# Experts ranked by token count: 20 with 64 places, 44 with 32 in four column tiles, and a row-wise first projection

## The reference

```python
s = sigmoid(t @ router_w); choice = s + router_bias
# groups of 8 experts: the 4 best of 8 groups, in them the TOP_K = 6 best experts of a token
w = take(s, eidx); w = w / sum(w) * 2.5
gates = sum(one_hot(eidx, 64) * w)
def expert_step(acc, p):
    wg, wu, wd, g = p
    hid = silu(t @ wg) * (t @ wu)              # 1024 -> 256
    return acc + (hid @ wd) * g[:, None], None # 256 -> 1024
shared = (silu(t @ sh_w_gate) * (t @ sh_w_up)) @ sh_w_down
return routed + shared
```

## Time and profile before

| | |
|---|---|
| Median of 3 runs | 1358.21 us (1357.56 to 1358.25) |
| Profiled execution | 1358.36 us, span 1356.6 us |
| TensorE busy | 1299.2 us, 96% |
| VectorE, ScalarE, GpSimd busy | 481.6, 324.2, 78.0 us |
| HBM read | 445.61 MB, 329 GB/s over the span |
| Gate and up matmuls, L925 | 446.5 us |
| Down matmuls, L947 | 233.8 us |
| Gather, L899 | 136.3 + 126.4 us |
| Scatter, L993 | 104.0 + 100.5 us |
| Mean granted TensorE clock | 0.989 |

### The profile page before, as it was taken

One profiled execution on the slowest core, in us unless ns is written; L12 is line 12 of the kernel. 1 busy time (PEld: TensorE's weight loads), 2 busy tenths in 40 slices (PEclk: granted clock), 3 DMA queues, 4 the chain that ended last, 5 costly groups with the idle time before them and its releaser, 6 DMA issues.

```text
span 1356.6 us, 17873 instructions
## 1 busy us (share of the span) xinstructions
PE 1299.2 (96%) x6452; PEld 707.9 (52%) x6452; DVE 481.6 (36%) x1079; ACT 324.2 (24%) x789; POOL 78.0 (6%) x100
## 2 busy tenths in 40 slices
PE   6988999999999999999799999999999999999995
PEld 3665744454444444544488857445544444445442
DVE  2385633333222333332422326333332223333324
ACT  1653212212121222221123222122121222221211
POOL 1333100000000000000140000000000000000000
PEclk9989999999999999999899999999999999999998
DMA  9334469999999999999861234599999999999991
GB/s 331 124 124 155 171 219 415 417 419 415 419 412 416 417 418 419 417 416 417 281 204 63 85 133 186 216 415 420 417 418 417 413 417 416 416 420 416 418 416 59
DMA packets 80323, 447.29 MB, mean 330 GB/s; under 512 B 7437, under 2 KB 25289, under 8 KB 30616
## 3 DMA queue, kind: packets, MB, share of 16 engines
q1 hardware_dynamic: 77264, 439.25, 80.0%
q0 software_dynamic: 1904, 6.46, 1.3%
q10 hardware_dynamic: 1112, 1.01, 0.2%
HBM read 445.61 MB, written 1.05 MB: 329 GB/s over the span
## 4 chain that ended last, share of the span: by engine, by line
PE 93%; issue 2%; DVE 2%; DMA 1%; ACT 1%; DVEq 0%; POOL 0%; POOLq 0%; SPq 0%
PE bank L925 33%; PE bank L947 17%; PE bank L899 10%; PE bank L993 9%; PE bank L785 4%; PE bank L749 4%; PE bank L853 2%; PE bank L662 2%; PE bank L788 2%; PE bank L935 2%; DMA ring<-in_l_w_in 1%; PE bank L962 1%; PE bank L891 1%; PE bank L644 1%; PE bank L628 1%
## 5 line engine op out<-in xcount | busy, mean ns | idle before, releaser
L925 PE MATMUL bank<-ring,big 128*64 128x512 f32 x2048 | 446.5, 594 | 0.1
L925 PEld LDWEIGHTS bank<-ring,big 128*64 128x64 f32 x2048 | 146.1, 137 | 277.9 <-issue 277.9
L947 PE MATMUL bank<-ring,big 128*64 128x512 f32 x1024 | 233.8, 598 | 2.2 <-ACT big L1205 2.2
L1601 DVE SCALAR_TENSOR_TENSOR ys_low<-bank,gcol,ys_high 128x512 fp32r<-128x512 f32 x128 | 96.1, 751 | 204.1 <-ACT ys_high L1211 204.1
L1593 DVE TENSOR_TENSOR big<-big,bank 128x256 f32<-128x256 f32 x64 | 27.0, 421 | 373.7 <-ACT big L1201 373.7
L899 PE MATMUL bank<-pick,xs_high 128*128 128x256 f32 x512 | 136.3, 301 | 0.0
L1211 ACT ACTIVATE ys_high<-bank,gcol 128x512 fp32r<-128x512 f32 x128 | 88.1, 688 | 192.1 <-PE bank L947 192.1
L947 PEld LDWEIGHTS bank<-ring,big 128*64 128x64 f32 x1024 | 67.8, 136 | 120.6 <-issue 109.6
L899 PE MATMUL bank<-pick,xs_low 128*128 128x256 f32 x512 | 126.4, 282 | 0.0
L1201 ACT ACTIVATE big<-bank 128x256 f32<-128x256 f32 x64 | 24.5, 383 | 405.7 <-PE bank L925 405.7
L899 PEld LDWEIGHTS bank<-pick,xs_high 128*128 128x128 f32 x512 | 97.6, 191 | 26.0 <-issue 24.8
(11 more groups left out here) (236 smaller groups left out, 1069.1 us busy)
## 6 DMA issues: line engine op xcount, KB each, us to landing
ring<-in_l_exp_w_gate SPq DMA_DIRECT2D x128, 1024.0 KB, 9.3
ring<-in_l_exp_w_up SPq DMA_DIRECT2D x128, 1024.0 KB, 11.4
ring<-in_l_exp_w_down SPq DMA_DIRECT2D x128, 1024.0 KB, 14.5
ring<-in_l_w_in SPq DMA_DIRECT2D x16, 1024.0 KB, 12.4
ring<-in_l_w_out SPq DMA_DIRECT2D x8, 1024.0 KB, 9.0
par<-in_l_ln_g POOLq DMA_DIRECT2D x4, 512.0 KB, 8.9
par<-in_l_ln_b POOLq DMA_DIRECT2D x4, 512.0 KB, 11.5
ring<-in_l_sh_w_gate SPq DMA_DIRECT2D x2, 1024.0 KB, 6.6
```

The source lines that it names most:

```text
L925: ins = mm(ps[SLOTS * q:SLOTS * q + SLOTS, :], xg[:, c, SLOTS * j:SLOTS * j + SLOTS], both[:, c], start=(c == 0), stop=(c == C - 1))
L947: ins = mm(ps[SLOTS * q:SLOTS * q + SLOTS, :], hidT[pr][:, m, SLOTS * q:SLOTS * q + SLOTS], wt[:, m, HALF * h:HALF * h + HALF], start=(m = ...
L1601: ins = v.scalar_tensor_tensor(ys[1][:, pr, part], ps[:], gcol[:, pr:pr + 1], ys[0][:, pr, part], ALU.mult, ALU.subtract)
```

## The change

- Experts are ranked on the chip by their number of tokens. Experts 0 to 7 stay in front in natural order, so that the first two groups need not wait for the ranking; the other 56 follow, largest first. `ranks` (VectorE) counts for each expert how many have a larger key and makes a permutation matrix; `sort` (TensorE) applies it to places, gates, expert numbers and keys during the first group; `ordered` (VectorE) copies out the result.
- The first 20 in this order, 5 groups (`first`, three `wide`, `turn`), keep 64 places. The other 44, 11 groups (`narrow`), get NSLOT = 32. A narrow group does gate and up of all four experts in one pass of four column tiles of 32, one down pass, 2 instead of 4 transposes, and 8 instead of 16 scatter matmuls. Its tokens are gathered 128 places wide, two pieces to a bank (`pairs`). `turn` computes wide and gathers for a narrow group.
- SyncE reads the expert numbers of the next group from `order` and loads those weights.
- A further round runs where an expert has more tokens than places.
- The groups other than narrow ones are written out instead of looped.
- The first projection's weights are loaded as four pieces, each two of the eight whole rows that a partition holds (11,520 contiguous bytes), and the latent projection accumulates over them as they land; the ring's layout before the loop is moved to suit, and two of the four `out0` loads wait for the last gate.
- Layer 1's input projection loads wait for the last narrow group's reads.

The core of the diff:

```diff
+NSLOT = 32
+NATURAL = 8
+KINDS = (("first", 1), ("wide", 3), ("turn", 1), ("narrow", 11))
...
+def last_use_of_weights(kind, j, w):
+    if kind == "narrow":
+        return "gu" if w < 2 else ("dn", 1)
     return ("gu", j // 2) if w < 2 else ("dn", j // 2, 1)
...
+            win = I["l0_w_in"].rearrange("(p c) n -> p (c n)", c=C)
+            for k in range(WPIECES):
+                cs = slice(WPIECE * k, WPIECE * k + WPIECE)
+                load(("in0", k), ring[:, cs], win[:, cs])
...
+                def refill(lp, experts):
+                    for j, w in IN_ORDER:
+                        lp.read(sp, last_use_of_weights(lp.kind, j, w))
+                        sp.dma_start(loop_weights(L, j, w), expert_weights(L, experts[j], w))\
+                          .then_inc(S(f"unit_full{loop_unit(L, j, w)[0]}"), 16)
+                def in_place(at):
+                    return [sp.value_load(order[0:1, bass.ds(at + j, 1)], min_val=0, max_val=NE - 1) for j in range(GE)]
...
+            for k in range(WPIECES):
+                unit_wait(pe, ("in0", k))
+                for tb in range(TB):
+                    ps = bank_open(pe, ("lat", tb)) if k == 0 else bank[banks.at[("lat", tb)][0]]
+                    for c in range(WCHUNKS * k, WCHUNKS * k + WCHUNKS):
+                        ins = mm(ps[:, 0:LAT], xT[:, c, P * tb:P * tb + P], win0[:, c, 2 * CONV:],
+                                 start=(c == 0), stop=(c == C - 1))
...
+                def sort(lp):
+                    lp.moved(pe, "rowsT")
+                    pe.wait_ge(S("perm"), L + 1)
+                    ps = lp.open(pe, "sorted")
+                    for tb in range(TB):
+                        mm(ps[:, P * tb:P * tb + P], routedT[:, tb, :], perm, start=True, stop=True)
+                    mm(ps[0:1, 2 * P:2 * P + NE], expert[0:NE], perm[0:NE, 0:NE], start=True, stop=True)
+                    ins = mm(ps[0:1, 3 * P:3 * P + NE], rank[0:NE, 1:2], perm[0:NE, 0:NE], start=True, stop=True)
...
+                def narrow(lp, last=False):
...
+                    ps = lp.open(pe, "gu")
+                    for j in range(GE):
+                        for w in range(2):
+                            weights_landed(lp, j, w)
+                    for c in range(C):
+                        for j in range(GE):
+                            u = loop_unit(L, j, 0)[0]
+                            both = ring[:, u * UNIT:(u + 2) * UNIT].rearrange("p (w c f) -> p c w f", w=2, c=C)
+                            r = slice(NSLOT * j, NSLOT * j + NSLOT)
+                            ins = mm(ps[r, :], xn[:, c, r], both[:, c], start=(c == 0), stop=(c == C - 1))
+                    lp.made(ins, "gu")
```

More of the change, by code:

```diff
@@ L56 @@
 GSLOT = GE * SLOTS
-MAXR = T // SLOTS
+MAXR = T // SLOTS + 1
 UNROLL = 2
+NSLOT = 32
+NATURAL = 8
+KINDS = (("first", 1), ("wide", 3), ("turn", 1), ("narrow", 11))
+BEGIN = {"first": 0, "wide": 1, "turn": 4, "narrow": 5}
+NWIDE = GE * BEGIN["narrow"]
+APART = 32768.0
 NEG = -1e30
@@ L169, in plan_banks @@
             u.add(("gather", L, c), GATHER_BANKS[c % 2])
[L170 to L176, removed]
+        wide = [("gT", 2)]
+        wide += [(("gu", pr), pr) for pr in range(GE // 2)]
+        wide += [(("hT", pr), pr) for pr in range(GE // 2)]
+        wide += [(("dn", pr, h), 2 + h) for pr in range(GE // 2) for h in range(2)]
+        scatter = [(("scatter", n), SCATTER_BANKS[n]) for n in range(4)]
+        gather = [(("gather", c), LOOP_GATHER[c]) for c in range(C)]
+        pair = [(("pair", c), PAIR_BANKS[c]) for c in range(C // 2)]
+        narrow = [("gT", 1), ("gu", 0), ("hT", 0)] + [(("dn", h), 2 + h) for h in range(2)] + pair
+        narrow += [(("scatter", n), 6 + n % 2) for n in range(4)]
+        times = dict(KINDS)
+        u.loop((L, "first"), wide + [("rowsT", 6), ("sorted", 7)] + gather + scatter, times["first"])
+        u.loop((L, "wide"), wide + gather + scatter, times["wide"])
+        u.loop((L, "turn"), wide + pair + scatter, times["turn"])
+        u.loop((L, "narrow"), narrow, times["narrow"], but=("pair",))
     return u
@@ L279, in run_groups @@
             group(lp)
[L280 to L286, removed]
+    lp.u = 0
+def last_use_of_weights(kind, j, w):
+    if kind == "narrow":
+        return "gu" if w < 2 else ("dn", 1)
     return ("gu", j // 2) if w < 2 else ("dn", j // 2, 1)
@@ L531, in prog_sync @@
-                lp = ExpertLoop(L, banks, S, bank)
-                with sp.Fori(1, NGRP) as i:
-                    lp.i = i
[L534 to L538, removed]
-                          .then_inc(S(f"unit_full{loop_unit(L, j, w)[0]}"), 16)
+                    early = range(3 * GE)
@@ L1229, in prog_scalar @@
                 for c in range(0, C, 2):
                     gathered(bank_read, bank_done, ("gather", L, c))
-                lp = ExpertLoop(L, banks, S, bank)
-                run_groups(act, lp, group)
+                wide(ExpertLoop(L, "first", banks, S, bank, i=0))
+                for i in range(dict(KINDS)["wide"]):
+                    wide(ExpertLoop(L, "wide", banks, S, bank, i=i))
+                wide(ExpertLoop(L, "turn", banks, S, bank, i=0))
+                lp = ExpertLoop(L, "narrow", banks, S, bank)
@@ L1586, in group, with wide @@
+                def wide(lp):
+                    after = "narrow" if lp.kind == "turn" else "wide"
+                    if lp.kind == "first":
+                        ranks()
                     lp.read(dve, "gT")
-                    if not last:
-                        select(lp, lp.groups(GE, GE), lp.count(2, 2, 1))
+                    select(lp, after, lp.groups(GE, GE), lp.count(2, 2, 1))
                     def hidden(pr):
                         ps = lp.read(dve, ("gu", pr))
-                        dve.wait_ge(lp.sem("silu"), lp.count(GE // 2, 0, pr + 1))
+                        dve.wait_ge(lp.own("silu"), lp.own_count(GE // 2, pr + 1))
```

464 lines of the change are left out of this document (326 added, 138 removed).

## The result

The changed kernel takes 1377.29 us (median of four runs, 1376.31 to 1377.44) against 1358.23 us for the kernel before in runs beside it (1357.56 to 1362.14). The ratio is 1.0133, with a 95% interval of 1.0116 to 1.0150: slower by 1.3%. The forecast was 1378. The profiled execution took 1376.31, its span 1374.5, which is 17.9 more than before.

What follows compares the result with a forecast made beforehand. TensorE was taken as the bound, with the DMA only 0.5 us in 30 behind. Narrow parts +23, ranking and turn +3 and first projection -5 on 1358.4 gave 1379, stated as 1378 us; range 1320 to 1402.

Steps and rivals of the forecast that it cites:

- Four tiles: Narrow gate and up: four column tiles share the array fully, 6.94 us at full clock instead of 13.88.
- Rival 3: Narrow gate and up: four tiles share the array less well than two; 1415 to 1463 us; chance 0.10.
- The circle: Narrow groups: all eight gate/up units are freed only at that stage's end, so the period is 22.8 us + G.
- G: Length of a narrow group's gate and up: 6.94 us at full clock, 9.7 us with the expected half clock.
- The clock: Narrow groups after the first restart at 1.2 GHz for 5.5 us, half of it lost: 2.75 us more gate and up.
- The period: From one narrow group to the next: 32.5 us, nine times per layer; 29.7 without the clock drop.
- The first period: First narrow group's start to the next: queue dry after 8.7 us, then eight loads, 29.6 us in all.
- The narrow part: First narrow gate and up to last scatter: 329.3 us before, 340.8 after; +11.5 per layer, +23 for both.
- The ranking: First group of each layer: added transposes, small matmuls and VectorE operations cost 1.9 us per layer, bounds 0.5 and 4.
- The turn group: Last wide group before the narrow ones: gives 0.4 us back in gathers.
- The first projection: Layer 0's start: weights in four row-wise pieces, first gate ending at 32 to 35.7; -5 us, bounds 0 and -9.
- Rival 1: Narrow groups: clock holds or recovers almost at once, DMA bound at period 29.7; 1323 us; chance 0.26.

Runs made afterwards that it cites:

- 22-filler kernel: The changed kernel with 22 extra matmul products, results unused, at the end of every narrow group but the last: 1357.96 us, ratio 0.9976 to the kernel before.
- pair kernel: The changed kernel with narrow gate and up done in two pairs of experts, the first pair's units refilled early: 1339.21 us, ratio 0.9838 to the kernel before.
- the fillers' products: The changed kernel with 44 extra 256-column products, results unused, at the end of every narrow group but the last: 1492.1 us, ratio 1.0969 to the kernel before.
- 10 fillers: The changed kernel with 10 extra matmul products, results unused, after the scatter of a narrow group: 1376.70 us, ratio 1.0128 to the kernel before.

## Why the prediction was right

The total is within a microsecond, and that closeness is luck: two misses cancel, and the forecast of 1378 stands 1.4 below the prediction's own sum without a reason given. The mechanism and the sign are not luck. The terms, in us against before, measured between the starts of the same steps in the two profiled executions:

| term | predicted | measured |
|---|---|---|
| up to the first gather | -5 | -5.1 |
| ranking, both layers | +3.8 | +7.6 |
| wide and turn groups, both layers | -0.8 | +1.5 |
| between the loops | 0 | -1.2 |
| narrow parts and what follows, both layers | +23 | +15.1 |
| sum | +21 | +17.9 |

- **Four tiles** share the array in full: 64 matmuls in 7.07 us are 110 ns each, where two tiles had 217 and the whole array 440. That is 4.0 times. The row's 721 ns is no contradiction: it is the mean length of one instruction, and they overlap. Rival 3 is out. The estimate of 3.2 times that the prediction took from the Trainium skill (TensorE: Matmul & The Clock Gate, "Measured speedup vs the span model") is below what this trace shows.
- **The circle.** Predicted 22.8 + G, measured 22.6 + G, at half clock and, with a lengthened stage, 22.6 in most periods at full clock. Breaking it brought the period to 29.82 us, near the predicted DMA limit of 29.7. This step is shown from three sides: its constant, its slope, and its removal. The constant holds for a G of some 8.4 us or more. In the 22-filler kernel G is 7.3 in the mean and the period 30.49, 23.2 more, because there the DMA limit and the circle lie on each other. The prediction has the condition for this the wrong way round: the downs' 10 us stay clear of the next loads when G + 2.8 is 10 or more, not 10 or less.
- **The clock** falls in every wait behind a narrow group, as the three restarts of before said; the stage loses 2.0 us on average (9.07 against 7.07), not 2.75. The Trainium skill's section "HAM oscillation — how this bites in real kernels", on the same page, describes a kernel whose bursts wait for DMA and restart at the lower clock each time. The trace agrees (some 11 us idle, with the clock at 0.50 at the end of each). With the clock held in most groups the span is 20.4 us shorter, more than the whole loss of 17.9.
- **The period** was predicted at 32.5 and is 31.69: nine of them are 7.3 us less per layer than forecast. The DMA moved 395 GB/s there (387 forecast), and TensorE was busy for 78% of the span, not some 70%. **The first period** was 29.6 and is 31.46. The sum counted on 8.7 us of queued work at the first narrow start. In fact its gate and up weights landed just then, at 335.45, so all four downs were still to move, and the DMA had a hole as in the 22-filler kernel. The windows of that period in the kernel after:

```profile
335.58:342.65 7.07, 7.07 (x65) 2.42 (x65) 0.49 (x2) 0.00 (x0) 0.00 (x0) 1.00 1.02 424
342.65:347.40 4.75, 4.75 (x44) 4.13 (x46) 1.27 (x3) 1.54 (x4) 0.00 (x0) 1.00 0.92 336
347.40:366.90 19.50, 5.68 (x38) 2.12 (x30) 5.03 (x9) 1.85 (x4) 0.00 (x0) 0.77 1.01 421
```

They move 3.00 + 1.60 + 8.21 = 12.8 MB, a whole group, which is 30.3 us at 423 GB/s, and the hole in the second window is 4.75 x (1 - 336 / 423) = 1.0.

- **The narrow part** from its first start to the work after the loop: before 335.27 us, after 342.82, so +7.5 against a predicted +11.5. Ten periods are 316.67 against 301.94, +14.7 (predicted +20.2); the last group and what follows it 26.15 against 33.33, -7.2 (predicted -8.7).
- **The ranking** is the term that was mis-sized the other way: 3.7 us in layer 0 and 3.9 in layer 1, where 1.9 was taken for each (the upper bound was 4). The step counted VectorE's own operations and left out whose bank the transposes need. Its excess of 3.8 us eats half of the 7.8 that the narrow parts gave back. The turn group ate 2.3 more: it was to give 0.4 per layer and cost 0.7, because the weights of the first narrow group landed 30.8 us after the turn's start (304.69 to 335.45).
- **The first projection** gave 5.1 us by the gather (predicted 5), its first gate ending at 34.19, within 32 to 35.7. The last piece landed at 24.18; the prediction said 23.4, and its own figures (20 us from 2.5) give 22.5. The matmuls on it took 3.06 us, over the 2.8 allowed, and the gate 6.91. Alone the change is worth 0.4%.
- **Rival 1** had the right pace for the pair kernel and the wrong total: 1339 and not 1323. Its period of 29.7 was nearly right (29.82). The profiled execution's span is 16.5 us less than before's, not 35 less. The narrow parts and what follows saved 10.5 and 11.6 us instead of 16.5 each, which is 10.9 of the 18.5 missing. The ranking is 4.0, the stretch up to the first gather 2.2 (2.8 us gained instead of 5, with the router and the shared expert partly at half clock), the work between the loops 1.7, less 0.3 in the wide groups.

## What to carry to other kernels

Where an engine's stage releases every buffer that its next run waits for, the period is stage plus latency plus loads, and utilisation of neither resource shows it. Release buffers piece by piece before making the stage faster: here a stage of 14 us of TensorE work with an early release beat the one of 7 us by 38 us, because a queued load covers both the latency and the slow restart. Where one engine leads by half a microsecond in thirty, price what bounds next before the edit; and for an added instruction, ask who last used its bank.

## What the runs showed of the hardware

- A plain float32 product was recorded as two instructions: the fillers' products with 256 columns as two of 217 ns each, 434 in all (1760 rows for 880 products), and gate and up of a narrow group, 8 x 4 = 32 products in the code, as 64. The scatter, in fp32r, has one for each product (L1140, 8 per narrow group). So "64 matmuls" in these pages and in the prediction are instructions, and the rows before the change showed it already.
- Four 32-column tiles ran at 110 ns per matmul instruction of 512 columns, where two tiles took 217 and the whole array 440.
- With 6.4 us without work per group (10 fillers) the clock dropped in all 20 groups that had this wait; with 2.2 us (22 fillers) in five of 22. After the drop the half clock lasted 10.3 to 13.6 us in the narrow groups listed above, and reached 4.4, 3.2 and 6.0 us into gate and up; half of that is what the three took over 7.07 us (2.2, 1.5, 3.0).
- With a group's gate and up weights in 16 loads of 0.5 MiB instead of 8 of 1 MiB, a single issue on SyncE's queue took 6.22 us and the DMA moved 409 GB/s in the mean of the narrow part; with loads of 1 MiB the pair kernel held 422.
